# More gate and up pairs by seven products, and two of their four weight sums added up by transfers from memory

## What is computed

```python
# first block, twice (DEPTH = 2); D_FF = 2816
h = rms_norm(x, norm_ffn_w[i])
g = jnp.einsum("bld,df->blf", h, w_gate[i])
u = jnp.einsum("bld,df->blf", h, w_up[i])
x = x + jnp.einsum("blf,fd->bld", jax.nn.silu(g) * u, w_down[i])
...
# second block, before and after the mixer
def swiglu_ffn(x, w_in, w_out):
    g, u = jnp.split(x @ w_in, 2, axis=-1)
    return (jax.nn.silu(g) * u) @ w_out
x = x + 0.5 * swiglu_ffn(rmsnorm(x, norm_ffn1[l]), ffn1_w_in[l], ffn1_w_out[l])
```

## Time and profile before

| | us |
|---|---|
| median of 3 runs | 2689.13 (2689.08 to 2689.93) |
| the profiled execution | 2689.1 |
| its span (first to last instruction) | 2687.3 |
| TensorE busy in it | 2642.6 |
| VectorE busy in it | 1821.6 |
| ScalarE busy in it | 1285.0 |

### The profile page before, as it was taken

The page is one execution under the profiler, slowest core; times in us unless marked ns, Lnnn a source line. Parts: engine busy times, 40 slices in busy tenths (PEclk is TensorE's granted clock), DMA queues, the critical chain, the costliest instruction groups (busy, mean ns, idle before and its releaser), DMA issues.

```text
span 2687.3 us, 37446 instructions
## 1 busy us (share of the span) xinstructions
PE 2642.6 (98%) x15123; PEld 2235.7 (83%) x15123; DVE 1821.6 (68%) x2738; ACT 1285.0 (48%) x1956; POOL 26.7 (1%) x45
## 2 busy tenths in 40 slices
...
GB/s 217 94 2 110 95 90 107 94 90 163 79 2 110 102 86 110 95 106 82 83 114 95 90 158 79 72 78 71 78 92 90 133 95 94 94 92 91 116 84 74
DMA packets 80429, 255.80 MB, mean 95 GB/s; under 512 B 9600, under 2 KB 12800, under 8 KB 79872
## 3 DMA queue, kind: packets, MB, share of 16 engines
...
## 4 chain that ended last, share of the span: by engine, by line
PE 89%; DVE 6%; ACT 4%; issue 1%; DMA 0%; DVEq 0%; SPq 0%; ACTq 0%
PE PS L1607 22%; PE PS L1608 22%; PE PS L1609 22%; PE PS L1636 4%; PE PS L1638 4%; PE PS L1637 4%; PE PS L1886 1%; DVE WLO L2419 1%; PE PS L1868 1%; ACT WHI L1974 1%; PE PS L1566 1%; PE PS L1655 1%; PE PS L1654 1%; PE PS L1656 1%; PE PS L1832 0%
## 5 line engine op out<-in xcount | busy, mean ns | idle before, releaser
L2419 DVE TENSOR_TENSOR WLO<-WR,WHI 128x1024 fp32r<-128x1024 f32 (+4 forms) x482 | 518.6, 1080 | 402.8 <-ACT WHI L1974 400.4
L1974 ACT CAST WHI<-WR 128x1024 fp32r<-128x1024 f32 (+4 forms) x482 | 448.4, 931 | 525.4 <-PE PS L1609 410.9
L1607 PE MATMUL PS<-HHI,WHI 128*128 128x512 f32 x1680 | 670.4, 399 | 0.9 <-ACT Z L2086 0.9
L1609 PE MATMUL PS<-HHI,WLO 128*128 128x512 f32 x1680 | 654.9, 390 | 0.0
L1608 PE MATMUL PS<-HLO,WHI 128*128 128x512 f32 x1680 | 654.9, 390 | 0.0
L1607 PEld LDWEIGHTS PS<-HHI,WHI 128*128 128x128 f32 x1680 | 315.9, 188 | 70.6 <-issue 5.0
L1609 PEld LDWEIGHTS PS<-HHI,WLO 128*128 128x128 f32 x1680 | 315.5, 188 | 66.9
L1608 PEld LDWEIGHTS PS<-HLO,WHI 128*128 128x128 f32 x1680 | 316.0, 188 | 66.1 <-issue 4.4
L1607 PE MATMUL PS<-FHI,WHI 128*128 128x512 f32 x693 | 269.6, 389 | 0.0
L1608 PE MATMUL PS<-FLO,WHI 128*128 128x512 f32 x693 | 269.6, 389 | 0.0
L1609 PE MATMUL PS<-FHI,WLO 128*128 128x512 f32 x693 | 269.6, 389 | 0.0
...
## 6 DMA issues: line engine op xcount, KB each, us to landing
WR<-in_stream SPq DMA_DIRECT2D x338, 512.0 KB, 3.3
...
WR<-in_stream SPq DMA_DIRECT2D x64, 320.0 KB, 2.9
...
X<-xkeep POOLq DMA_DIRECT2D x24, 256.0 KB, 5.6
...
X<-in_xin SPq DMA_DIRECT2D x8, 256.0 KB, 5.7
```

Source lines behind the costliest of these rows:

```text
L1607: e.matmul(out, hi[:, i, :], xhi, start=first, stop=False)
L1609: t = e.matmul(out, lo[:, i, :], xhi, start=False, stop=final)
L1974: e.copy(hi, raw).then_inc(S["act_high"], 1)
L2419: e.tensor_tensor(lo, raw, hi.bitcast(F32), ALU.subtract).then_inc(S["dve_low"], 1)
```

## The change

1. **Pairs.** SEVEN becomes a table: pairs 5 to 14, 16, 17, 18, 20, 21 (15 pairs), in the third stage (f = 2) 8 to 14, 16, 17, 18, 20, 21 (12). So 57 of 88 pairs go by seven instead of 36, and most stand in rows without a pair by eight between them.
2. **Sums.** Of the four sums two are now a weight block fetched from memory by SyncE ("tget") onto which GpSimd has a second block added by a transfer with accumulation ("tadd"), 256 KB each. Sum 0 (tile TS, at the same address as the TLO that it later becomes) is needed by the two others, which VectorE makes with two instructions ("tsum", lines 2532 and 2533). Sum 1 (tile WS, at the address of WLO) is split into the free first half of the up block's slot ("thib", "tlob"), whose own first half is no longer loaded or split. Sum 1 is used in u = 5.
3. **Waits.** "tget" of a pair waits until the accumulation of the pair before has landed, and for sum 0 until u = 1 of the pair two before (in SEVEN) has read the buffer. "tadd" waits for its "tget", "tsum" for the landing of "tadd" 0, "thib" for that of "tadd" 1.
4. **Products.** u = 1 and u = 2 change places; THI, TLO and P1 are double buffers by pair; "thi" and "tlo" are single instructions of 1536 columns; the second "snap" goes to PSUM, and "gs" and "cc" become one instruction of 512 columns each.
5. Some semaphores are merged to make room; no step moves by that.

In the diff `added(q, f, j, 0)` waits on s_sum[0] for the pair; "tadd" is in GpSimd's function, "tget" in SyncE's; PAIR_COUNT numbers the pairs by seven through all stages.

```diff
-SEVEN = range(5, FT, 2)
-PRODUCTS = ((0, 0, True), (1, 0, True), (2, 0, True), (0, 1, False), (0, 0, False), (1, 0, False), (2, 0, False))
+SEVEN = {f: (*range(5 if f != 2 else 8, 15), 16, 17, 18, 20, 21) for f in range(4)}
+PRODUCTS = ((0, 0, True), (2, 0, True), (1, 0, True), (0, 1, False), (0, 0, False), (1, 0, False), (2, 0, False))
...
+ADDING = 3.0
...
     def weight_sums(self, f, j):
         yield from self.added(("sslo", f, 3))
         last = max(k for k, pair in self.pair_of.items() if pair == (f, j))
+        used = two_before(f, j)
+        if used is not None:
+            yield from self.added(("srow", f, used, 1, 3))
+            yield from self.until(("srow", f, used, 1, 3))
+        self.add("tget", f, j, 0)
+        yield self.add("tadd", f, j, 0)
+        self.spawn(self.last_sum(f, j, last))
+        yield ADDING
         while last - RAW not in self.low:
             yield 0.1
-        yield self.add("tsum", f, j)
+        if used is not None:
+            yield from self.added(("srow", f, used, 3, 3))
+            yield from self.until(("srow", f, used, 3, 3))
+        done = self.add("tsum", f, j)
+        self.load_due()
         self.advance()
...
+    def last_sum(self, f, j, last):
+        while self.used + SPL <= last:
+            yield 0.1
+        self.add("tget", f, j, 1)
+        yield self.add("tadd", f, j, 1)
+        yield ADDING
+        yield self.add("thib", f, j)
+        self.add("tlob", f, j)
...
                     elif u == 1:
-                        q.wait_ge(S["dve_xlow"], n["tlo", f, j, 1])
+                        q.wait_ge(S["dve_xlow"], n["tlo", f, j])
...
                     elif u == 5:
+                        q.wait_ge(S["dve_xlow"], n["tlob", f, j])
                         q.wait_ge(S["dve_gs"], n["pd", f, j])
...
-                settle(e.tensor_tensor(WT[0][:, 0, :], gate[:, 0:T], up[:, 0:T], ALU.add))
-                e.tensor_tensor(WT[1][:, 0, :], up[:, 0:T], up[:, T:2 * T], ALU.add)
-                settle(e.tensor_tensor(WT[0][:, 1, :], WT[0][:, 0, :], up[:, T:2 * T], ALU.add))
-                e.tensor_tensor(WT[1][:, 1, :], WT[0][:, 1, :], gate[:, T:2 * T], ALU.add).then_inc(S["dve_scale"], 1)
+                added(q, f, j, 0)
+                settle(e.tensor_tensor(t2, t1, up[:, T:2 * T], ALU.add))
+                e.tensor_tensor(t4, t2, gate[:, T:2 * T], ALU.add).then_inc(S["dve_scale"], 1)
...
+            elif kind == "tadd":
+                f, j, i = a
+                k_gate, k_up = o.slot_of["seven", f, j]
+                q.wait_ge(s_get[i], 16 * PAIR_COUNT[f, j] + 16)
+                block = weights_from(k_up)[:, T:2 * T] if i else weights_from(k_gate)[:, 0:T]
+                e.dma_start(block_sum(f, j, i), block, accum_op=ALU.add).then_inc(s_sum[i], 16)
...
+            elif kind == "tget":
+                if i == 1:
+                    q.wait_ge(S["pe_slot"], k_up - SPL + 1)
+                elif two_before(f, j) is None:
+                    q.wait_ge(S["dve_xlow"], n["sslo", f, 3])
+                else:
+                    q.wait_ge(S["pe_prod"], o.product_end[f, two_before(f, j), 1])
+                if PAIR_COUNT[f, j]:
+                    q.wait_ge(s_sum[i], 16 * PAIR_COUNT[f, j])
+                e.dma_start(block_sum(f, j, i), weights_from(k_up)[:, 0:T]).then_inc(s_get[i], 16)
```

More of the change, by code:

```diff
@@ L57 @@
     **dict.fromkeys(["root", "hroot", "rroot", "roroot", "croot"], "rooted"),
-    **dict.fromkeys(["hlo", "flo", "ylo", "yls", "sslo", "tlo"], "xlow"),
-    **dict.fromkeys(["hhi", "fhi", "yhi", "yhs", "sshi", "thi"], "xhigh"),
+    **dict.fromkeys(["hlo", "flo", "ylo", "yls", "sslo", "tlo", "tlob"], "xlow"),
+    **dict.fromkeys(["hhi", "fhi", "yhi", "yhs", "sshi", "thi", "thib"], "xhigh"),
 }
@@ L217, with two_before @@
                 ((1, 2), (1, 3), (2, 1), (3, 1)), ((2, 2), (3, 2), (2, 3), (3, 3)))
+PAIR_COUNT = {p: i for i, p in enumerate((f, j) for f in SEVEN for j in SEVEN[f])}
+def two_before(f, j):
+    i = SEVEN[f].index(j)
+    return SEVEN[f][i - 2] if i >= 2 else None
 class Order:
@@ L277, in load, with load_due @@
     def load(self):
-        if self.next_load < len(self.slots):
+        self.due += 1
+        self.load_due()
+    def load_due(self):
+        while self.due and self.next_load < len(self.slots):
+            before = self.pair_of.get(self.next_load - RAW)
+            if before and not self.summed(before):
+                return
             self.add("load", self.next_load)
             self.next_load += 1
+            self.due -= 1
     def advance(self, look=LOOK):
@@ L524, in ffn @@
         m = NORM_FFN[f]
-        for pair in SEVEN:
+        for pair in SEVEN[f]:
             at_ = self.slots.index((gate, i, 0, DT, pair * P, P))
             self.pair_of[at_] = self.pair_of[at_ + 1] = (f, pair)
+            self.halved.add(at_ + 1)
         self.x["sv", f] = list(self.x_now)
@@ L582, in seven @@
         self.slot_of["seven", f, j] = slots
-        self.run(lambda: ("tlo", f, j, 1) in self.n)
         for u in range(7):
+            if u == 1:
+                self.run(lambda: ("tlo", f, j) in self.n)
+            elif u == 5:
+                self.run(lambda: ("tlob", f, j) in self.n)
             for r in range(4):
@@ L621, in weight_sums @@
         last = max(k for k, pair in self.pair_of.items() if pair == (f, j))
+        used = two_before(f, j)
[6 more added lines that the diff above has]
+        yield ADDING
         while last - RAW not in self.low:
             yield 0.1
-        yield self.add("tsum", f, j)
-        self.advance()
-        if j - 2 in SEVEN:
-            yield from self.until(("srow", f, j - 2, 5, 3))
-        for k in range(2):
-            self.add("thi", f, j, k)
-        for k in range(2):
-            yield ("thi", f, j, k)
-            self.add("tlo", f, j, k)
+        if used is not None:
+            yield from self.added(("srow", f, used, 3, 3))
+            yield from self.until(("srow", f, used, 3, 3))
+        done = self.add("tsum", f, j)
+        self.load_due()
+        self.advance()
+        yield done
+        yield self.add("thi", f, j)
+        self.add("tlo", f, j)
+    def last_sum(self, f, j, last):
[6 more added lines that the diff above has]
+        self.add("tlob", f, j)
     def last_tile(self, f, down, i, j):
@@ L1458, in combination, with weights_from, added, block_sum @@
         return SUMS[k][:, :, :].rearrange("p r t -> p (r t)")
+    def weights_from(k):
+        size = o.slots[k][3] * o.slots[k][5]
+        return stream[offset[k]:offset[k] + P * size].rearrange("(p n) -> p n", p=P)
+    def added(q, f, j, i):
+        q.wait_ge(s_sum[i], 16 * PAIR_COUNT[f, j] + 16)
+    def block_sum(f, j, i):
+        return WS[:, o.slot_of["seven", f, j][1] % SPL, 0:T] if i else TS[:, SEVEN[f].index(j) % 2, 0, :]
+    def first(f, j):
+        return P1[SEVEN[f].index(j) % 2][:, :]
+    def sums(f, j):
+        b = SEVEN[f].index(j) % 2
+        return (x[:, b, :, :].rearrange("p u c -> p (u c)") for x in (TS, THI, TLO))
     def block_weights(f, j, u):
```

165 lines of the change are left out of this document (93 added, 72 removed).

## The result

| | before | after |
|---|---|---|
| median, us | 2689.4 (2689.08 to 2689.93, 4 runs) | 2980.64 (2979.2 to 2982.14, 4 runs) |
| span of the profiled execution | 2687.3 | 2979.8 |

The ratio is 1.1083 (95% interval 1.1064 to 1.1102): 10.8% slower. The prediction had the direction, but 2779 us and a range up to 2895; the loss is 291 us where it said 90.

The account below looks back on a forecast made before the run. TensorE was taken as the bound, 2642.6 of 2687.3 us. Gain -29.0, stops +108.8 and clock +10 made +89.8 on 2689.1, so 2778.9 us; range 2686 to 2895.

Parts of the forecast that it names:

- The gain of 29.0 us: On TensorE: 17.6 us from 57 pairs by seven instead of 36, plus 11.4 from the third stage's pairs 5 and 7.
- The 9.7 for the third stage: Pairs 5 and 7 by eight there: 11.4 us of excess time gone, less 1.7 for two pairs by eight.
- L = 6.0: Time from a sum's fetch issue to its accumulation's landing: fetch 2.9, accumulation 3.0, handovers 0.1 us.
- upper bound of 9.2: Longest L considered: 3.3 for a 512 KB load, 5.6 for a transfer on GpSimd's queue among others, 0.3 more.
- the prediction's own formula: Stops summed for a given L; the slow-accumulation rival had L = 9.2, stops 230.6, 2890.7 us; chance 0.18 for 2830 to 2900.
- The start of the row at pair 5: Pair 6's fetch waits for pair 5's accumulation, two L in series: TensorE stops 8.6 us for pair 5's tlo.
- the next stop: After the row start at pair 5, pair 7's sum lands late and TensorE stops 4.8 us more.
- VectorE's prices: Start-to-start times of VectorE steps by column count, 0.34 us for 256 to 1.67 for 1536; 9.3 us a round.
- round of 10.5: VectorE's and ScalarE's steps inside a row of sevens take 10.5 us, 0.4 slower than TensorE's 10.07.
- Clock: Half clock on TensorE after stops of about 2 us or more: 0 to 34 us over some 20 stops, 10 taken.
- What would show it: Signs: TensorE waiting for TLO at pair 5 and the snap at u = 3; VectorE's longest waits for TS landing.

Follow-up runs that it names:

- e15: e13 with the first pair of a row behind one by eight (5, 16, 20) also written in a new order: 2675.5 us.
- e8: Kernel before the change, with pairs 9, 11, ... 21 by seven in the third stage instead of 5, 7, ... 21: 2677.72 us.
- e4: Changed kernel, with the second transfer of each sum overwriting the block instead of being added to it: 2886.65 us.
- e6: Changed kernel with one number changed, the planner's assumed time for a sum's transfers (ADDING) 10.0 instead of 3.0: 2792.4 us.
- e14: The 57 pairs with the same fixed order inside rows as e13, but all four sums by VectorE: 2702.41 us.
- e13: The 57 pairs, sum 0 by VectorE, only sum 1 by transfers, 10 us assumed; VectorE's and ScalarE's steps inside rows in a fixed order: 2701.99 us.
- e12: Changed kernel, with 16 unused matmuls on TensorE in rows just before it waits for the first snap: 3001.35 us.
- e1: Changed kernel's sums by transfers, but pairs by seven again 5, 7, ... 21 in every stage: 2952.85 us.
- e5: e1 with one number changed, ADDING 10.0 instead of 3.0: 2709.57 us.

## Why the prediction was wrong in size

- **The gain of 29.0 us: right.** e15 is at 2675.5 with 14.0 of stops and slow pace; without them 2661.5, against the 2660.1 that the prediction gave. The 9.7 for the third stage by itself were measured as 11.2 (e8).
- **L = 6.0: mis-sized.** It measured 9.1 (median, sum by sum), near its upper bound of 9.2. The fetch took 3.8, not 2.9; the accumulation 4.8, not 3.0; the handover 0.3, not 0.1, which no row had shown. One wrong choice was to let the second operand of the addition "cancel": e4 prices it at 1.0 to 1.7 us. It was not the only one: without the addition L was still 7.2. The figure of the Trainium skill (DMA: Bandwidth & Descriptors, section "Anatomy of one DMA — SWDGE (gpsimd) path") for a transfer without an addition on GpSimd's queue gave an estimate of 2.6 for 256 KB; e4's plain transfers there took 3.1, the accumulations 4.1 and 4.8. The prediction used it for the fetch too, which goes over SyncE's queue and took 3.8.
- **By the prediction's own formula L = 9.2 gives 2890.7,** so 90 us are missing besides L. The fetch was set at the end of u = 1 of the pair two before. It was issued 0.2 to 15.8 us after that and the landing of the pair before (median 5.8 of 49 sums), behind a load waiting for tsum and low. In 17 sums it was also issued within 0.5 us of the other sum's, and there L was 9.3 to 11.4, median 10.7. The prediction saw both queues in the order and charged them only at the start of the row and at pair 18.
- **The start of the row at pair 5:** 8.6 us of stop forecast, 11.44 measured in the first stage (e6: 9.6), 11.9 in the second, but only some 5 in the fourth. The serial double L was right: the two sums took 6.8 and 7.8 us one behind the other. That the next stop was 4.80 where 4.8 was forecast is luck: "ww" of pair 5 came some 6 us later than forecast, and TensorE, by the larger first stop and slow pace, as much later.
- **VectorE's prices: right.** The prediction's list gives 9.3 us of work a pair, 10.5 with two more instructions of 0.61; e14 measured 10.51. Its round of 10.5 for the changed order was not a floor: written in another order the work, with one instruction of VectorE more, runs in 10.08 (e13).
- **Clock: 10 us, measured 71.7 of slow pace more.** The working counted 20 stops; there were 53. In the rounds from pair 6 to 9 e12 shows that it lay inside the wait for the landings: there it is a part of the account of the 291 us but not a cause. Elsewhere what it costs is open.
- **The step that failed most is the missing rival.** The prediction took the order as given and asked whether the sums land in time for TensorE. The diff held the answer to another question: the planner assumes ADDING = 3.0, the prediction itself had L between 5.3 and 9.2, and VectorE and ScalarE, which work in order, pay that difference while all behind it waits. With 10.0 in its place 188 of the 291 us go in the changed kernel (e6) and nearly all of the loss when pairs alternate (e1 against e5). Much of the rest of e6 is order too, by its trace.
- **What would show it** named TensorE's waits for TLO at pair 5 (6 us or more in three stages), the snap at u = 3 and VectorE's for TS. The first holds in two stages of three, the second in full. The third is there with 185.1 us, but VectorE's largest sum of waits is another, 298.9 us for WHI, which was 400.4 before. ScalarE's wait for WS, with 284.2 us the largest of VectorE's and ScalarE's for a landing, was not named.

Left open: why sum 0 takes 10.7 us when both fetches go out together (its place behind the other, the issue on GpSimd of 0.86 and then 1.12 us, the weight loads, or the memory); no run separated these. Two fetches at once are not enough: at pair 5, where sum 0 is first in both queues and no weight load runs beside it, they go out 0.4 us apart and it takes 6.8. e14 against e13 doesn't tell what longer rows would cost.
